# Other start addresses modulo 512 bytes for the weight buffers of a two-block transformer kernel

## The chip, the cores and the metric

The kernel runs on one core of a Trainium2 chip. The metric is the device time of one execution in microseconds (us). A partition of the on-chip memory (SBUF) is addressed in bytes; all addresses below are byte addresses within a partition, and "modulo 512" is the remainder that such an address leaves.

## The reference, cut to what matters

Two transformer blocks are computed for 256 tokens of width 1024, in float32, all of it in one launch. The first has a layer of gated spatial mixing beside latent attention, a layer of retention, and two SwiGLU networks of width 2816. The second has, twice, a SwiGLU of width 4096, a mixer of three branches (a gated delta rule, two banded attentions), and another SwiGLU of width 4096. By far the most work are matrix products of the 256 tokens with weights:

```python
def swiglu(h, w_gate, w_up, w_down):
    return (jax.nn.silu(h @ w_gate) * (h @ w_up)) @ w_down
```

## The kernel before, in words

**Weights.** All weights come as 772 chunks of at most 128 x 1024 float32 (512 KB), in the order in which TensorE uses them (the list `ORDER`). SyncE loads chunk c into slot c % 6 of `raw` (line 3269). ScalarE copies it, rounded to the short float32 format of TensorE (`float32r`), into slot c % 5 of `whi` (`upper`, line 1244). VectorE subtracts `whi` from `raw` and writes the rest, the lo part, into slot c % 5 of `wlo` (`lower`, line 2004). TensorE waits for `wlo` of the chunk, and ScalarE overwrites a slot only when TensorE has finished the chunk that stood there. A slot of `whi` or `wlo` has 4096 bytes, so all slots have the same start modulo 512; a block of 128 columns, which is what one weight load reads, has 512 bytes.

**Activations.** They are split in the same way. `xx` holds the normalised input of a product as 8 tiles k of 128 features, each with a hi part and a lo part of 256 tokens (1024 bytes each). `H` holds up to 32 such tiles of hidden values. `RX` is a third buffer of that kind, for the products that start before the layer norm's statistics are there; its hi and lo parts are 288 values apart and 258 columns of each are used. `Hs` is `H` shifted by 64 bytes, for the last down projection alone.

**Matmuls.** Every matmul goes through `mm`, and the profile gives all of them line 452. A matmul has a weight load of its own, of 128 columns of the stationary operand, and streams the other operand, the moving one. There are three forms:

- The pair (`mm2`): with the hi weights stationary, the hi and the lo part of a tile are streamed at once, 512 columns. Then, with the lo weights stationary, the hi part, 256 columns. It serves nearly all of the gate, up and down products of the SwiGLUs (`gemm_wide`, and the loop at line 679). The two halves of the result are added by VectorE.
- The triple (`mm3`): 256 columns three times, hi weights by hi part, lo weights by hi part, hi weights by lo part, all onto the same 256 columns of the result. It serves the projections of the mixers (`gemm_fm`, `gemm_acc`, `gemm_last`) and, with 258 columns from `RX`, the first products after a layer norm (`gemm_raw`).
- Token-major products (`gemm_tm`, `value`, `down_tokens`): the activations are stationary, and the weights are streamed, 512, 384 or 324 columns.

While a matmul streams its moving operand, the load of the next matmul's stationary operand runs beside it. So in a pair the lo weights are loaded while 512 columns from the start of an `xx` or `H` tile are streamed, and the next hi weights while 256 columns from the same start are streamed.

**Addresses.** `lay_memory` (line 242) places the buffers one behind the other. `line(p)` puts in a gap so that the next buffer starts at p modulo 512. All sizes of the buffers in question are multiples of 512 bytes. Before the change `raw` and `whi` start at 0 modulo 512, and `wlo`, `x`, `xx`, the scratch `t12` and `H` at 64. `Hs` starts 64 bytes behind `H`. `RX` starts 65664 bytes behind `H`, which is 128 modulo 512, its tiles k are 2304 bytes apart (256 modulo 512), and its lo part is 1152 bytes behind the hi part (128 modulo 512).

Of the kernel before, what the change touches and what calls it, by code (L numbers as in the profile page):

```python
# [7 lines left out]
F32R = mybir.dt.float32r  # L8
# [5 lines left out]
NRAW, NHL, CW = 6, 5, 1024  # L14
# [227 lines left out]
def lay_memory(nc, ctx, plan):  # L242
    m = Memory()

    def sb(name, shape, dt=F32):
        return ctx.enter_context(nc.sbuf_tensor(name, shape, dt))

    def line(past=0):

        gap = (past - nc.sbuf_base) % 512  # L250
        if gap:
            sb(f"gap{nc.sbuf_base}", [128, gap // 4])
        return nc.sbuf_base
# [13 lines left out]
    m.onc = nc.alloc_sbuf_tensor_at("onc", [128, 1], F32R, offset=on, align_bytes=64)[:, :]  # L267
    m.onr = m.onc.broadcast_to([128, 128])
    m.onm = m.onc.bitcast(F32).broadcast_to([128, 128])
    line(0)  # L270
    m.raw = sb("raw", [128, NRAW, CW])
    line(0)
    m.whi = sb("whi", [128, NHL, CW], F32R)
    line(64)
    m.wlo = sb("wlo", [128, NHL, CW], F32R)
    line(64)
    m.x = sb("x", [128, 8, 256])
    line(64)
    m.xx = sb("xx", [128, 8, 2, 256], F32R)
    m.xh, m.xl = m.xx[:, :, 0, :], m.xx[:, :, 1, :]  # L280
    at = line(64)
    t12 = sb("t12", [128, 2048 + 128])
    m.t1, m.t2 = (t12[:, 1024 * i:1024 * i + 1024].rearrange("p (a b) -> p a b", b=256) for i in range(2))
    blk = nc.alloc_sbuf_tensor_at("blk", [128, NBLK + 128], F32R, offset=at, align_bytes=64)
    m.pair = nc.alloc_sbuf_tensor_at("pair", [128, 256], F32R, offset=at + 6144, align_bytes=64)[:, :]
    m.E, m.eye16 = blk[:, 0:NBLK], blk[:, NBLK - 128:NBLK].bitcast(F32)
    m.Ph, m.Pl = blk[:, NBLK - 128:NBLK], blk[:, NBLK:NBLK + 128]
    at = line(64)
    left = nc.sbuf_bytes_remaining
    nar = min((left() if callable(left) else left) // 4 - 8 - 4096, 21696)  # L290
    region = sb("region", [128, 4096 + nar])
# [2985 lines left out]
def emit(nc, ins, out, plan):  # L3277

    with ExitStack() as ctx:
        m = lay_memory(nc, ctx, plan)  # L3280
        block = ctx.enter_context(nc.Block())

        @block.sync
        def _(e):
            sync_program(e, m, ins, out)

        @block.scalar
        def _(e):
            scalar_program(e, m, ins)

        @block.vector
        def _(e):
            vector_program(e, m)

        @block.gpsimd
        def _(e):
            gpsimd_program(e, m, ins)

        @block.tensor
        def _(e):  # L3300
            tensor_program(e, m)

        tables = {n: g.at for n, g in m.sig.items()}
        assert plan is None or plan == tables
        return tables
# [147 lines left out]
```

## Time and profile before

| | us |
|---|---|
| median of 3 runs | 2266.87 |
| lowest and highest | 2266.55, 2266.92 |
| the profiled execution's own time | 2266.66 |
| its span, first to last instruction | 2264.9 |
| TensorE busy in the span | 2251.1 |
| VectorE busy | 1781.2 |
| ScalarE busy | 1285.3 |

The profiled execution is a run of its own beside the three; 1.8 us of its time lie outside the span. "Busy" of TensorE is the union of all matmuls in flight, which overlap each other, so the mean duration of a matmul is not what it costs. What one costs is the distance from its start to the next one's start.

### The profile page before, as it was taken

To read this page: it belongs to the slowest core of one execution; us is meant where nothing else is said; L and a number is where in the kernel's file an instruction comes from. 1 tells how busy PE (TensorE), PEld (TensorE's weight loads), DVE (VectorE), ACT (ScalarE), POOL (GpSimd) and SP (SyncE) were. 2 spreads that over 40 slices of the span, in tenths; PEclk is the share of its full clock that TensorE was granted. 3 is DMA by queue.
4 is the path that set the end of the run, shared out by engine and by line. 5 is a ranking of instruction groups with operands and counts; after the bars stand their busy time and mean duration, and the time that the engine had idled before them with its cause. 6 is when DMAs were issued, how large, how long until landed. Compare 5 with 4: busy or idle time off the path is not lost.

```text
span 2264.9 us, 37643 instructions
## 1 busy us (share of the span) xinstructions
PE 2251.1 (99%) x15119; PEld 2047.7 (90%) x15119; DVE 1781.2 (79%) x2713; ACT 1285.3 (57%) x2016; POOL 79.4 (4%) x96
## 2 busy tenths in 40 slices
PE   9999999999999999999999999999999999999998
PEld 8988889998888888999999888998889999998887
DVE  7899658879858876897679886698768976798854
ACT  7855455655445555585666554466545856565542
POOL 0022000002100000020000000000000200000000
PEclk9999999999999999999999999999999999999999
DMA  7466565456556665654455555566665543556663
GB/s 244 132 199 196 193 211 176 150 159 215 184 186 214 195 192 191 204 178 129 133 172 193 197 194 190 168 203 206 195 194 197 180 133 122 182 182 221 190 185 100
DMA packets 115084, 412.45 MB, mean 182 GB/s; under 512 B 12896, under 2 KB 14304, under 8 KB 114656
## 3 DMA queue, kind: packets, MB, share of 16 engines
q1 hardware_dynamic: 114480, 407.77, 55.9%
q8 instruction: 120, 1.97, 0.4%
q0 software_dynamic: 288, 2.10, 0.3%
q14 instruction: 52, 0.43, 0.1%
q10 hardware_dynamic: 144, 0.18, 0.0%
HBM read 408.96 MB, written 1.05 MB: 181 GB/s over the span
## 4 chain that ended last, share of the span: by engine, by line
PE 88%; DVE 8%; ACT 2%; issue 1%; DMA 0%; SPq 0%; POOL 0%; DVEq 0%; ACTq 0%
PE ps L452 87%; DVE wlo L2004 3%; DVE region L2796 1%; ACT whi L1244 1%; ACT region L1466 1%; DMA raw<-in_ew_c 0%; PE ps L715 0%; DVE region L2323 0%; DVE RX L2193 0%; DVE x L2051 0%; DVE region L2326 0%; DVE x L2200 0%; DVE region L2439 0%; DVE region L2466 0%; DVE region L2965 0%
## 5 line engine op out<-in xcount | busy, mean ns | idle before, releaser
L452 PE MATMUL ps<-xx,whi 128*128 128x512 f32 (+1 forms) x4504 | 1286.2, 352 | 3.2 <-DVE wlo L2004 2.2
L2004 DVE TENSOR_TENSOR wlo<-raw,whi 128x1024 fp32r<-128x1024 f32 (+3 forms) x772 | 925.2, 1207 | 266.7 <-ACT whi L1244 265.7
L1244 ACT ACTIVATE whi<-raw 128x1024 fp32r<-128x1024 f32 (+3 forms) x772 | 801.1, 1043 | 491.3 <-PE ps L452 481.1
L452 PE MATMUL ps<-xx,wlo 128*128 128x256 f32 x3696 | 1025.0, 277 | 0.0
L452 PEld LDWEIGHTS ps<-xx,whi 128*128 128x128 f32 x4504 | 794.4, 188 | 120.2 <-issue 2.8
L452 PEld LDWEIGHTS ps<-xx,wlo 128*128 128x128 f32 x3696 | 693.8, 188 | 0.4
L452 PE MATMUL ps<-H,whi 128*128 128x512 f32 (+1 forms) x2144 | 571.6, 338 | 0.1
L452 PE MATMUL ps<-H,wlo 128*128 128x256 f32 x1632 | 453.7, 278 | 0.0
L452 PEld LDWEIGHTS ps<-H,whi 128*128 128x128 f32 x2144 | 370.7, 188 | 45.1 <-issue 0.6
L452 PEld LDWEIGHTS ps<-H,wlo 128*128 128x128 f32 x1632 | 306.7, 188 | 0.1
L1999 DVE TENSOR_REDUCE t<-ps 128x256 f32<-128x512 f32 x320 | 219.5, 688 | 31.6 <-PE ps L452 31.2
L1393 ACT ACTIVATE H<-t 128x256 fp32r<-128x256 f32 x140 | 58.6, 419 | 81.2 <-DVE t L2353 31.9
L1428 ACT ACTIVATE t<-t 128x256 f32<-128x256 f32 x160 | 65.5, 410 | 64.9 <-DVE t L2395 35.8
L452 PE MATMUL ps<-region 128*128 128x128 f32 (+9 forms) x944 | 89.4, 272 | 0.0
L452 PE MATMUL ps<-RX,whi 128*128 128x258 f32 x480 | 88.9, 284 | 0.0
L452 PEld LDWEIGHTS ps<-region 128*128 128x128 f32 (+5 forms) x944 | 75.8, 158 | 6.7
L452 PE MATMUL ps<-whi,Hs 128*128 128x512 f32 x256 | 79.8, 392 | 0.0
L452 PE MATMUL ps<-whi,xx 128*128 128x512 f32 (+1 forms) x288 | 79.3, 360 | 0.0
L452 PEld LDWEIGHTS ps<-RX,whi 128*128 128x128 f32 x480 | 75.3, 190 | 0.2
L3170 POOL TENSOR_TENSOR t<-t,R 128x256 f32<-128x256 f32 x44 | 53.3, 1211 | 549.1 <-ACT t L1428 549.1
L2022 DVE TENSOR_TENSOR H<-t,H 128x256 fp32r<-128x256 f32 x150 | 62.2, 419 | 9.0 <-ACT H L1393 5.8
L452 PE MATMUL ps<-RX,wlo 128*128 128x258 f32 x240 | 68.0, 283 | 0.0
(316 smaller groups left out, 1592.4 us busy)
## 6 DMA issues: line engine op xcount, KB each, us to landing
raw<-in_sg SPq DMA_DIRECT2D x128, 512.0 KB, 4.2
raw<-in_su SPq DMA_DIRECT2D x128, 512.0 KB, 4.2
raw<-in_sd SPq DMA_DIRECT2D x128, 512.0 KB, 4.4
raw<-in_mw_g SPq DMA_DIRECT2D x48, 512.0 KB, 3.7
raw<-in_fg SPq DMA_DIRECT2D x44, 512.0 KB, 4.1
raw<-in_fu SPq DMA_DIRECT2D x44, 512.0 KB, 4.2
raw<-in_fd SPq DMA_DIRECT2D x32, 512.0 KB, 3.6
raw<-in_mw_a SPq DMA_DIRECT2D x24, 512.0 KB, 4.2
```

What stands on the lines that cost most here:

```text
L452: return e.matmul(out, lhsT, rhs, start=start, stop=stop, skip_group_check=True)
L1244: e.activation(m.whi[:, c % NHL, 0:cw], m.raw[:, c % NRAW, 0:cw], ACT.Copy).then_inc(s["whi"].h, s["whi"].up(c))
L1393: e.activation(H[:, j, 0, :], m.t2[:, j % 4, :], ACT.Copy, scale=-0.5 if raw(j) else 1.0).then_inc(s["hhi"].h, s["hhi"].up(st, j))
L1428: e.activation(g, g, ACT.Silu).then_inc(s["silu"].h, s["silu"].up(st, j))
L1466: e.activation(S[:, i, sl], S[:, i, sl], ACT.Exp, bias=st[:, 1, c:c + 1], accum_out=st[:, 2, c:c + 1]).then_inc(s["aact"].h, s["aact"].up( ...
L1999: return e.tensor_reduce(dst, b[:, :].rearrange("p (a b) -> p b a", a=2), AX, ALU.add)
L2004: e.tensor_tensor(m.wlo[:, c % NHL, 0:cw], m.raw[:, c % NRAW, 0:cw], m.whi[:, c % NHL, 0:cw].bitcast(F32), ALU.subtract).then_inc(s["wlo"] ...
L2022: e.tensor_tensor(dst, src, hi.bitcast(F32), ALU.subtract).then_inc(s[sig[1]].h, s[sig[1]].up(*key))
L2796: e.scalar_tensor_tensor(y[:, d:256], pr[:, 0:256 - d], pk(f"cw{l}", 12 * (3 - d) + i), y[:, d:256], ALU.mult, ALU.add).then_inc(s["cdve"] ...
L3170: e.tensor_tensor(g, g, m.R[:, 0, :], ALU.mult).then_inc(s["fnrm"].h, s["fnrm"].up(st, j))
```

## The change

The order of the weight buffers becomes `raw`, `wlo`, `whi`. `raw` follows the constants with no gap, `wlo` starts at 128 modulo 512 and `whi` at 320. The `x`, `xx`, `t12` and `H` buffers start at 0. Relative to `xx` and `H`, `wlo` moves from 0 to +128 bytes, and `whi` from -64 to -192 bytes (320 - 512). No instruction, wait or transfer is added, removed or moved; only addresses differ.

```diff
--- before.py
+++ after.py
@@ -267,25 +267,24 @@
     m.onc = nc.alloc_sbuf_tensor_at("onc", [128, 1], F32R, offset=on, align_bytes=64)[:, :]
     m.onr = m.onc.broadcast_to([128, 128])
     m.onm = m.onc.bitcast(F32).broadcast_to([128, 128])
+    m.raw = sb("raw", [128, NRAW, CW])
+    line(128)
+    m.wlo = sb("wlo", [128, NHL, CW], F32R)
+    line(320)
+    m.whi = sb("whi", [128, NHL, CW], F32R)
     line(0)
-    m.raw = sb("raw", [128, NRAW, CW])
+    m.x = sb("x", [128, 8, 256])
     line(0)
-    m.whi = sb("whi", [128, NHL, CW], F32R)
-    line(64)
-    m.wlo = sb("wlo", [128, NHL, CW], F32R)
-    line(64)
-    m.x = sb("x", [128, 8, 256])
-    line(64)
     m.xx = sb("xx", [128, 8, 2, 256], F32R)
     m.xh, m.xl = m.xx[:, :, 0, :], m.xx[:, :, 1, :]
-    at = line(64)
+    at = line(0)
     t12 = sb("t12", [128, 2048 + 128])
     m.t1, m.t2 = (t12[:, 1024 * i:1024 * i + 1024].rearrange("p (a b) -> p a b", b=256) for i in range(2))
     blk = nc.alloc_sbuf_tensor_at("blk", [128, NBLK + 128], F32R, offset=at, align_bytes=64)
     m.pair = nc.alloc_sbuf_tensor_at("pair", [128, 256], F32R, offset=at + 6144, align_bytes=64)[:, :]
     m.E, m.eye16 = blk[:, 0:NBLK], blk[:, NBLK - 128:NBLK].bitcast(F32)
     m.Ph, m.Pl = blk[:, NBLK - 128:NBLK], blk[:, NBLK:NBLK + 128]
-    at = line(64)
+    at = line(0)
     left = nc.sbuf_bytes_remaining
     nar = min((left() if callable(left) else left) // 4 - 8 - 4096, 21696)
     region = sb("region", [128, 4096 + nar])
```

## Rows read from the trace of the kernel before

**Rows 1.** The page: span, TensorE busy time, TensorE clock in 40 slices.

```profile
span 2264.9 us, 37643 instructions
...
PE 2251.1 (99%) x15119; PEld 2047.7 (90%) x15119; DVE 1781.2 (79%) x2713; ACT 1285.3 (57%) x2016; POOL 79.4 (4%) x96
...
PEclk9999999999999999999999999999999999999999
```

**Rows 2.** Groups by line and shape, TensorE: busy us, mean ns, idle before.

```profile
L452 PE MATMUL ps<-xx,whi 128*128 128x512 f32 x2880 | 982.4, 390 | 0.0
...
L452 PE MATMUL ps<-H,whi 128*128 128x512 f32 x1120 | 381.2, 389 | 0.0
L452 PE MATMUL ps<-xx,whi 128*128 128x256 f32 x1616 | 301.7, 284 | 3.2 <-DVE wlo L2004 2.2 <-DVE xx L2059 1.1
L452 PE MATMUL ps<-H,whi 128*128 128x256 f32 x1024 | 190.4, 282 | 0.1
L452 PE MATMUL ps<-RX,whi 128*128 128x258 f32 x480 | 88.9, 284 | 0.0
L452 PE MATMUL ps<-whi,Hs 128*128 128x512 f32 x256 | 79.8, 392 | 0.0
...
L452 PE MATMUL ps<-whi,xx 128*128 128x512 f32 x160 | 50.4, 396 | 0.0
```

**Rows 3.** Waits of TensorE: us in total, times, longest.

```profile
PE ps L452 <- DVE wlo L2004: 2.2, 5, 1.0
```

**Rows 4.** Timeline of TensorE, a pair stretch: start us, us, instruction.

```profile
600.00 0.39 PE L452 MATMUL ps<-xx,whi 128*128 128x512 f32 x1
600.23 0.28 PE L452 MATMUL ps<-xx,wlo 128*128 128x256 f32 x1
600.34 0.39 PE L452 MATMUL ps<-xx,whi 128*128 128x512 f32 x1
...
610.43 0.28 PE L452 MATMUL ps<-H,wlo 128*128 128x256 f32 x1
```

**Rows 5.** Timeline of the weight loads in the same stretch.

```profile
600.00 0.19 PEld L452 LDWEIGHTS ps<-xx,wlo 128*128 128x128 f32 x1
```

**Rows 6.** Timeline of TensorE, a triple stretch on H.

```profile
1180.92 0.28 PE L452 MATMUL ps<-H,wlo 128*128 128x256 f32 x1
...
1191.17 0.28 PE L452 MATMUL ps<-H,wlo 128*128 128x256 f32 x1
```

**Rows 7.** Timeline of TensorE, a triple stretch on RX.

```profile
1460.77 0.28 PE L452 MATMUL ps<-RX,wlo 128*128 128x258 f32 x1
...
1461.13 0.28 PE L452 MATMUL ps<-RX,wlo 128*128 128x258 f32 x1
...
1461.48 0.28 PE L452 MATMUL ps<-RX,wlo 128*128 128x258 f32 x1
...
1461.85 0.28 PE L452 MATMUL ps<-RX,wlo 128*128 128x258 f32 x1
...
1471.93 0.28 PE L452 MATMUL ps<-RX,wlo 128*128 128x258 f32 x1
```

**Rows 8.** Timeline of TensorE, tokens against moving weights, xx stationary.

```profile
311.79 0.40 PE L452 MATMUL ps<-wlo,xx 128*128 128x512 f32 x1
...
326.55 0.40 PE L452 MATMUL ps<-wlo,xx 128*128 128x512 f32 x1
```

**Rows 9.** Timeline of TensorE, the same with Hs stationary.

```profile
2230.99 0.39 PE L452 MATMUL ps<-wlo,Hs 128*128 128x512 f32 x1
...
2248.33 0.39 PE L452 MATMUL ps<-wlo,Hs 128*128 128x512 f32 x1
```

**Rows 10.** Busy time by stretch: the pair stretch, then the triple stretch on H.

```profile
600.00:700.00 100.00, 100.00 (x591) 88.66 (x590) 66.74 (x91) 46.70 (x61) 1.29 (x1) 1.00 0.59 191
...
1180.50:1191.70 11.20, 11.20 (x97) 11.20 (x97) 11.20 (x26) 9.68 (x21) 0.00 (x0) 1.00 0.62 216
```

**Rows 11.** Groups of VectorE in the pair stretch, 600 to 700 us.

```profile
L2004 DVE TENSOR_TENSOR wlo<-raw,whi 128x1024 fp32r<-128x1024 f32 x31 | 37.9, 1222 | 27.0 <-ACT whi L1244 26.9
```

## The prediction

> **What bounds the kernel now.** I read the page first: TensorE is busy for 2251.1 of 2264.9 us, its clock is granted in full (2.4 GHz) in every slice [rows 1]. Then its waits: the longest in total, for lo weights, is 2.2 us [rows 3]. So nothing that feeds TensorE counts for much, and the time is the sum of the distances between matmul starts. The change touches no instruction. It can act only if the distance from one start to the next depends on where the operands lie.
>
> The groups by shape give the counts [rows 2]: 2880 + 1120 = 4000 pairs; (1616 + 1024)/2 = 1320 triples on xx and H, as each has two matmuls with hi weights; 480/2 = 240 triples on RX; token-major matmuls of 512 columns, three for every two with hi weights: 384 with Hs and 240 with xx stationary. The timelines give the distances, from the first to the last row and the number of repeats between (a row with x2 is two matmuls):
>
> - pair: 610.43 - 600.23 = 10.20 us for 30, **0.340 us** [rows 4]; 768 columns, so 0.443 ns per column.
> - triple on H: 10.25 us for 29, **0.3534 us** [rows 6]; also 768 columns.
> - triple on RX: 11.16 us for 31, **0.360 us** for 774 columns [rows 7].
> - token-major on xx: 14.76 us for 63 matmuls, **0.2343 us** for 512 columns [rows 8].
> - token-major on Hs: 17.34 us for 75, **0.2312 us** [rows 9].
>
> These sum to 1360 + 466 + 86 + 56 + 89 = 2057 us. The other 194 us of TensorE's busy time are matmuls on other tiles, other widths and the few waits; I cost the change on them at nothing, and leave them for the width of the range.
>
> **What can be gained.** The pair's rate is the fastest of the five. At 0.443 ns per column a triple would take 0.340, an RX triple 0.343 and a 512-column matmul 0.2267 us. The rest is excess: 1320 x 0.0134 = 17.7 us, 240 x 0.017 = 4.2 us, 240 x 0.0076 = 1.8 us, 384 x 0.0045 = 1.7 us, in all 25.4 us. In the pair the half of 512 columns is streamed beside a load at distance 0 (lo weights minus xx or H, modulo 512) and the half of 256 beside one at -64. The load of the lo weights starts together with the stream of the 512 [rows 4, 5]. The two halves take 0.23 and 0.11 us [rows 4], the same rate per column at two different distances. So I take the pair to be at its floor, and what can be gained is 25 us at most, 1.1%.
>
> **The change part by part.** Distances from the start of the moving operand to the start of what is loaded beside it, before and after, modulo 512:
>
> - Pair: lo load 0, becomes +128; hi load -64, becomes -192. Price unknown. From below: nothing, as it is at its floor. From above: the nearest rows in which 512 columns are streamed beside a load at +128 are those on Hs (Hs is 64 above H, hi weights 64 below it: +128 for two of three, +64 for the third), which cost 0.0045 us or 2.0% above the floor [rows 9]. On the pairs that would be 1360 x 0.020 = +27 us. With the 3.4% of xx [rows 8] it would be +46 us. I take nothing: the two halves of the pair show no difference between 0 and -64, and the token-major form on xx, where one load in three stands at the 0 that is free in the pair, has the larger excess of the two, so that the excess seems to belong to the form more than to the distance.
> - Triples on xx and H: the loads stand at 0, -64, -64 and become +128, -192, -192. These very distances are in the trace, in the RX triples: tile k of RX starts 128 + 256k above H, so the lo load there is at +128 for odd k and at -128 for even k, the first hi load at -192 for even k. What they show can be read in two ways. Per column, RX is slower (0.465 ns against 0.460). Per started 64 bytes (16 columns) it is faster: 258 columns touch 17, so 0.120 us is 7.06 ns each, as in the pair (0.340 over 48 is 7.08), while on H 0.3534 over 48 is 7.36. By the second reading a triple at the new distances loses its whole excess, -17.7 us; by the first it gains 0.005 ns x 768 x 1320, +5 us. The second gives one figure for two forms, and I lean to it, but its step at 258 columns rests on this one width. Between -17.7 and 0 I take half, -9 us.
> - RX: its distances become 0 or 256, 192 or -64, 64 or -192. The distances alternate with k by 256 already now, and the triples take 0.36, 0.35, 0.37 us in turn [rows 7] with no step of two, so I take nothing.
> - Token-major: the load of xx goes from +64, 0 to +192, -128, that of Hs from +128, +64 to +256, -64. Ends: -3.5 us (all of both excesses), and another 2% of 145 us, +3 us. I take 0.
> - Conversions: raw and whi both start at 0 now, and will not; the VectorE subtraction takes 1222 ns for a chunk [rows 11]. Cover: in the pair stretch VectorE is busy for 66.74 of 100 us [rows 10], so a subtraction could become half as long again before it bounds. In the triple stretch on H it is busy for all of 11.20 us [rows 10], but this work is run ahead by up to five slots. Without that cover each per cent on 772 subtractions of 1.2 us would be 9 us at the very most. I take 0.
> - The gaps and the order of the buffers by themselves: nothing, since no engine's work depends on them.
>
> Sum: -9 us. Against the profiled execution, 2266.66 (its span of 2264.9 and 1.8 us around it), that is 2257.7; the median of the runs is 0.2 us higher. I say 2258.
>
> The Trainium skill speaks against any effect: SBUF — State Buffer, "Who interferes with whom", states that only the port pair that VectorE and GpSimd share causes contention, and that TensorE has two independent read ports, for the moving operand and for the weight load. If that is all, start addresses move nothing and the sum is 0; it is weighed as the first rival.
>
> **The rivals.**
>
> 1. **No effect, 2266.9.** The triple could simply be bound by its loads. It has three loads in 0.3534 us, 0.118 each [rows 6], and the pair two in 0.340. If a load after a load costs 0.118 wherever it lies, the excess stays. For it: rows 6 and 7 are close (0.118 and 0.120), and rows 7 don't alternate with k. Against it: a bound by loads alone would give H and RX the same distance, and the same form (512 columns, ample time for the load) gives 0.2343 on xx and 0.2312 on Hs, whose distances differ by 64 bytes; something there depends on the address. The rule of the skill quoted above would give this case.
> 2. **Slower, 2294.** The pairs leave their floor. Stream and load would then collide at +128 and at -192 as they may do on Hs, and the stream is held up by 2.0%: +27 us. It decides as soon as a pair takes over 0.3422 us, since 4000 x 0.0022 is the 9 us of my gain; over 0.3411 the kernel is already slower if the triples gain nothing. For it: 0 and -64 are the two distances at which the pair is free, all others that the trace has come with an excess, and the pairs are 60% of the time. Against it: the larger excess of the two token-major forms is the one with a load at 0.
> 3. The conversions become the bound in the mixers: a part of the chance of slower, worth a few us.
>
> That the change does nothing because addresses end up elsewhere than it says is very unlikely: the line helper computes gaps from the actual base.
>
> **How the numbers follow.** Faster by the triples: 0.42, from 2241 (all 25.4 us) to 2262. No effect, which includes small gains and losses that cancel: 0.26. Slower: 0.32, of which most lies at +5 to +30 us. A difference of 0.2%, 4.5 us, is about what a measurement can tell from none. The range must take in both signs: 2243 leaves out the last 2 us of the full gain, 2296 holds the price of rows 9 on the pairs and leaves out that of rows 8. The faster case's own range is 2243 to 2262.
>
> **What the changed profile would show.** If right: a pair stretch still at 0.340 us per pair, triples on xx and H between 0.340 and 0.350, counts as before, no new waits of TensorE. If rival 1: all five distances as now. If rival 2: pairs at 0.343 to 0.350, which 30 pairs of a timeline tell at once. The conversions would show as longer rows of the subtraction and a wait of TensorE for lo weights far over 2.2 us. My forecast is wrong in its mechanism if the time falls while the triples stay at 0.353, or if the pair falls below 0.340.

## The result and the profile after

| | before | after |
|---|---|---|
| median, us | 2266.89 (6 runs) | 2309.45 (6 runs) |
| lowest and highest | 2266.55, 2272.03 | 2307.01, 2312.57 |
| profiled execution's own time | 2266.66 | 2312.57 |
| its span | 2264.9 | 2310.8 |
| TensorE busy | 2251.1 | 2296.7 |

The change makes the kernel slower: ratio 1.0186, 95% interval 1.0173 to 1.0199, 42.6 us on the medians. I had forecast 2258 us in a range of 2243 to 2296, with a chance of 0.32 for slower; 2309.45 lies outside the range. The profiled execution is at the upper end of the runs.

The page of the changed kernel, as in [rows 1]:

```profile
span 2310.8 us, 37643 instructions
...
PE 2296.7 (99%) x15119; PEld 2078.0 (90%) x15119; DVE 1786.1 (77%) x2713; ACT 1287.1 (56%) x2016; POOL 79.9 (3%) x96
...
PEclk9999999999999999999999999999999999999999
```

Instruction counts and clock are as before. The whole of the time is in TensorE's busy time, +45.6 of +45.9 us. The groups by line and shape, which answer to [rows 2] (the line numbers are one less after the change):

```profile
L451 PE MATMUL ps<-xx,whi 128*128 128x512 f32 x2880 | 1014.8, 394 | 0.0
...
L451 PE MATMUL ps<-H,whi 128*128 128x512 f32 x1120 | 393.6, 393 | 0.0
L451 PE MATMUL ps<-xx,whi 128*128 128x256 f32 x1616 | 302.7, 286 | 3.7 <-DVE wlo L2003 2.0 <-DVE xx L2058 1.5
L451 PE MATMUL ps<-H,whi 128*128 128x256 f32 x1024 | 191.0, 285 | 0.1
L451 PE MATMUL ps<-RX,whi 128*128 128x258 f32 x480 | 88.6, 284 | 0.0
```

Here is a way to read the cost of a pair from one row. The matmul of 512 columns is in flight for 394 ns (mean), longer than a whole pair takes, so the busy time of its group covers the pair stretches without a hole: busy time over count is the distance between pairs. On xx that is 982.4/2880 = 0.341 us before and 1014.8/2880 = 0.352 after, on H 381.2/1120 = 0.340 and 393.6/1120 = 0.351. Together +32.4 and +12.4, 44.8 us: the pairs are the whole loss. The triples' rows are up by 1.6 us together, RX is down by 0.3.

The waits of TensorE for lo weights, as in [rows 3], and VectorE's subtraction in the stretch of [rows 11]:

```profile
PE ps L451 <- DVE wlo L2003: 2.0, 4, 1.0
```

```profile
L2003 DVE TENSOR_TENSOR wlo<-raw,whi 128x1024 fp32r<-128x1024 f32 x28 | 34.3, 1225 | 28.4 <-ACT whi L1243 28.4
```

Neither moved. Then the timeline of the same pair stretch as [rows 4], the starts of five successive matmuls of 512 columns:

```profile
606.03 0.40 PE L451 MATMUL ps<-xx,whi 128*128 128x512 f32 x1
...
606.39 0.39 PE L451 MATMUL ps<-xx,whi 128*128 128x512 f32 x1
...
606.73 0.40 PE L451 MATMUL ps<-xx,whi 128*128 128x512 f32 x1
...
607.09 0.39 PE L451 MATMUL ps<-xx,whi 128*128 128x512 f32 x1
...
607.43 0.40 PE L451 MATMUL ps<-xx,whi 128*128 128x512 f32 x1
```

In the stretch of [rows 4] these starts were 0.34 us apart without exception. Now they are 0.36, 0.34, 0.36, 0.34: the pairs alternate. The section on patterns takes this up. In the tables that follow, a distance between starts is taken from all records of a form in the trace, each counted from its own start to the next matmul's start. They hold 4008 pairs: the 4000 of [rows 2], and eight more whose weights have 32 columns.

| form, sum of distances, us | before | after |
|---|---|---|
| pairs, 512-column half | 910.2 | 928.0 |
| pairs, 256-column half | 454.5 | 481.8 |
| triples on xx and H | 481.3 | 482.9 |
| triples on RX | 89.6 | 89.3 |
| token-major, 512 columns | 145.3 | 144.9 |

### The profile page after: what moved, and what is told of

Same layout as the page of the kernel before. It is cut to its first block, busy times and chain, and to the rows that moved or that the text cites. A ratio compares the mean times of both kernels' runs of the same rounds, so it can differ in the third digit from the quotient of the medians.

```text
span 2310.8 us, 37643 instructions
## 1 busy us (share of the span) xinstructions
PE 2296.7 (99%) x15119; PEld 2078.0 (90%) x15119; DVE 1786.1 (77%) x2713; ACT 1287.1 (56%) x2016; POOL 79.9 (3%) x96
## 4 chain that ended last, share of the span: by engine, by line
PE 88%; DVE 9%; ACT 2%; issue 1%; DMA 0%; SPq 0%; POOL 0%; DVEq 0%; ACTq 0%
PE ps L451 87%; DVE wlo L2003 3%; DVE region L2795 1%; ACT whi L1243 1%; DVE x L2199 0%; DMA raw<-in_ew_c 0%; PE ps L714 0%; ACT region L1465 0%; DVE region L2322 0%; DVE RX L2192 0%; DVE x L2050 0%; DVE region L2325 0%; DVE x L2221 0%; DVE region L2964 0%; DVE region L2431 0%
## 5 line engine op out<-in xcount | busy, mean ns | idle before, releaser
L451 PE MATMUL ps<-xx,whi 128*128 128x512 f32 (+1 forms) x4504 | 1319.6, 355 | 3.7 <-DVE wlo L2003 2.0
L451 PE MATMUL ps<-xx,wlo 128*128 128x256 f32 x3696 | 1039.3, 281 | 0.0
L451 PE MATMUL ps<-H,whi 128*128 128x512 f32 (+1 forms) x2144 | 584.6, 341 | 0.1
L451 PE MATMUL ps<-H,wlo 128*128 128x256 f32 x1632 | 458.5, 281 | 0.0
```

What stands on the lines that cost most here:

```text
L451: return e.matmul(out, lhsT, rhs, start=start, stop=stop, skip_group_check=True)
```

## The experiments

### One buffer at a time

Theory A: each half of a pair pays for the distance of the load beside it. Theory B: the two loads are coupled, and leaving either of the old distances costs the whole. Theory C: the distance of the hi weights does it all. Both kernels keep the changed order and gaps; all other buffers start at 0.

```diff
 (lo weights alone moved)
     line(128)
     m.wlo = sb("wlo", [128, NHL, CW], F32R)
-    line(320)
+    line(448)
     m.whi = sb("whi", [128, NHL, CW], F32R)
```

> The changed kernel with the hi weights put back to -64 from xx and H; only the lo weights stand at their new +128. In the changed kernel the pair takes 0.351 us against 0.340, and of these 11 ns about 4.5 lie in the half of 512 columns (beside which the lo weights are loaded) and about 7 in the half of 256 (beside which the hi weights are loaded). Theory A, each half pays for the distance of the load beside it: only the 512 half is longer, pair 0.345, time 2267 + 4000 x 0.0045 = 2285 us. Theory B, the two loads are coupled, and leaving either of the two old distances costs the whole: pair 0.351, 2309 us. Theory C, the lo distance is harmless and the hi distance does it all: 2267 us.

```diff
 (hi weights alone moved)
-    line(128)
-    m.wlo = sb("wlo", [128, NHL, CW], F32R)
     line(320)
     m.whi = sb("whi", [128, NHL, CW], F32R)
     line(0)
+    m.wlo = sb("wlo", [128, NHL, CW], F32R)
+    line(0)
```

> The changed kernel with the lo weights put back to 0 from xx and H (and behind the hi weights, as before the change); only the hi weights stand at their new -192. Theory A: only the half of 256 columns is longer, by 7 ns, pair 0.347, time 2267 + 28 = 2295 us. Theory B: pair 0.351, 2309 us. Theory C: 2309 us.

| | time, us | ratio to before | 512 half | 256 half |
|---|---|---|---|---|
| before | 2267.05 | | 0.2271 | 0.1134 |
| lo alone at +128 | 2288.96 | 1.0089 (1.0074 to 1.0104) | 0.2287 | 0.1184 |
| hi alone at -192 | 2303.99 | 1.0159 (1.0141 to 1.0176) | 0.2323 | 0.1175 |
| both (the change) | 2309.45 | 1.0186 (1.0173 to 1.0199) | 0.2315 | 0.1202 |

(The last two columns are mean distances between starts, in us, in the profiled execution.) Each move does harm by itself, +22 and +37 us, and the two together cost 43, not 59. All three theories fall. Against A: moving only the lo weights lengthens above all the 256-column half (by 5.0 ns), beside which the hi weights are loaded, at an unchanged distance. Against B: there are intermediate values. Against C: the lo weights alone cost 22 us.

### Order and absolute address

> The changed kernel's order of buffers (raw without a gap, lo weights ahead of hi weights) with the old distances: lo weights at 0 and hi weights at -64 from xx and H, everything 64 bytes further on modulo 512 than before. If only the distances between stationary and moving operands count (A, B and C alike): pair 0.340, 2267 us. If the order, the start of raw or absolute addresses have a part in the loss: above 2275 us.

```diff
     line(128)
     m.wlo = sb("wlo", [128, NHL, CW], F32R)
-    line(320)
+    line(64)
     m.whi = sb("whi", [128, NHL, CW], F32R)
-    line(0)
+    line(128)
     m.x = sb("x", [128, 8, 256])
 ...
```

The median is 2269.53 us, ratio 1.0003 (0.9991 to 1.0014), but no execution took that: five of the ten took 2266.9 to 2267.0 us and five 2272.1 to 2272.5. The kernel before has the same two levels, five of the thirteen executions beside it at the upper one; the section on the period of 256 comes back to them. The profile is one of the lower level and has the pairs at 0.340. The new order, `raw` without a gap and a shift of everything by 64 bytes cost nothing within that interval; the 43 us come from the distances.

### The grid of distances

```python
def pairs(lo, hi, reps=3, X=X):
    for _ in range(reps):
        b = bank()
        for k in range(8):
            c = k * 128
            mm(b[:, :], hi[:, c:c + 128], X[:, k].rearrange("p a b -> p (a b)"), k == 0, False)
            mm(b[:, 0:256], lo[:, c:c + 128], X[:, k, 0, :], False, True)
...
for i in range(8):
    for j in range(8):
        pairs(lo[i], hi[j])
```

> No part of the reference is computed: TensorE alone runs matmuls on prepared buffers while the other engines rest. For each of 8 x 8 combinations of start addresses modulo 512 in steps of 64 bytes (lo weights, hi weights; the moving operand at 0) it runs 24 pairs, then for each of 8 distances 24 matmuls of 512 and 24 of 256 columns with a load each, then 16 triples for each of the 64 combinations, and at last 48 pairs each at the old and the new distances with everything moved on by 64. Theory A: the time of a pair is a sum of one term for the lo distance and one for the hi distance; 0.340 at (0, -64), 0.351 at (+128, -192), 0.345 and 0.347 with one of the two moved; few other combinations are at 0.340. Theory B: 0.340 at a few combinations, 0.351 at all others, no intermediate values. If contention with VectorE and ScalarE was the cause, all combinations take 0.340 here, since those engines rest. If the absolute address counts, the last 48 + 48 pairs differ from the same distances in the grid.

First, matmuls of 512 columns alone, 24 in a row, each with a load of its own; the letters A to F behind `hi` are distances of 0, 64, 128, 192, 256 and 320 bytes. The timeline merges each run into one row: start, duration, count.

```profile
582.57 5.63 PE L179 MATMUL ps<-X,hiA 128*128 128x512 f32 x24
588.03 5.76 PE L179 MATMUL ps<-X,hiB 128*128 128x512 f32 x24
593.63 5.74 PE L179 MATMUL ps<-X,hiC 128*128 128x512 f32 x24
599.21 5.67 PE L179 MATMUL ps<-X,hiD 128*128 128x512 f32 x24
604.72 5.61 PE L179 MATMUL ps<-X,hiE 128*128 128x512 f32 x24
610.17 5.76 PE L179 MATMUL ps<-X,hiF 128*128 128x512 f32 x24
```

The starts of these runs are 5.46, 5.60, 5.58, 5.51 and again 5.45 us apart, over 24: 0.2275, 0.2333, 0.2325, 0.2296, 0.2271 us per matmul. Only TensorE is at work here, so no other engine's access can be the cause, and only the start of the weights differs from run to run: a stream is held up by the load beside it, by an amount that depends on their distance and repeats after 256 bytes. At distance 0 the 512 columns run at the rate of the pair, [rows 4], and 64 bytes further they take 2.5% more.

Matmuls of 256 columns with a load each behave otherwise:

```profile
626.85 3.02 PE L179 MATMUL ps<-X,hiA 128*128 128x256 f32 x24
629.70 2.99 PE L179 MATMUL ps<-X,hiB 128*128 128x256 f32 x24
632.53 3.01 PE L179 MATMUL ps<-X,hiC 128*128 128x256 f32 x24
```

These starts are 2.85 and 2.83 us apart, 0.1188 and 0.1179 us per matmul. At all eight distances it is 0.1175 to 0.1196; none reaches the 0.1134 of the pair's half of 256. So a 256-column matmul can be faster between other matmuls than among its like, and its time is not set by the distance of its own load alone.

Second, the pairs. The old distances (lo 0, hi 448 modulo 512) and the new ones (lo 128, hi 320), a lo matmul and the twentieth after it:

```profile
105.86 0.28 PE L179 MATMUL ps<-X,loA 128*128 128x256 f32 x1
...
112.66 0.28 PE L179 MATMUL ps<-X,loA 128*128 128x256 f32 x1
```

```profile
222.86 0.28 PE L179 MATMUL ps<-X,loC 128*128 128x256 f32 x1
...
229.86 0.28 PE L179 MATMUL ps<-X,loC 128*128 128x256 f32 x1
```

6.80 and 7.00 us, 0.340 and 0.350 a pair, with every other engine at rest. Moving everything by 64 bytes changed neither by more than 0.2 ns. The values are no sum of a term for each distance, as theory A has it: from lo 0 to lo 64 a pair goes from 340.0 to 346.6 ns at hi 192, and from 353.5 to 346.6 at hi 0. Over the 64 combinations the map repeats within 0.1 ns when the lo weights move by 256 bytes. When the hi weights do, it repeats within 0.2 ns for lo 0 and 64, but for lo 128 and 192 up to 3.6 ns lie between two such values (lo 128: hi 0 at 350.2, hi 256 at 346.6). The next section finds both values at one combination, after different starts. Third, the map of the triples modulo 256, in ns per triple (16 triples each, the first four left out):

```
triples         hi 0    hi 64   hi 128  hi 192
lo 0            360.0   353.3   355.0   353.3
lo 64           353.3   353.2   356.8   356.7
lo 128          357.1   354.8   356.2   346.7
lo 192          353.3   340.0   350.0   353.3
```

The old distances (lo 0, hi 192 modulo 256) give 353.3 and the new ones (lo 128, hi 64) 354.8, as in the whole kernel. And there is a combination at 340.0: the triple is not bound by its three loads.

One value of the grid did not fit. Lo 0, hi 320, the distances of the kernel with the hi weights alone moved, ran at 340.0 in the grid, while that kernel took 350 for most pairs. But that kernel's trace has the same loop over the same H in both ways. First the down projection at 1400 us, then the one at 1440; start of a lo matmul and of the thirtieth after it:

```profile
1399.74 0.28 PE L451 MATMUL ps<-H,wlo 128*128 128x256 f32 x1
...
1410.24 0.28 PE L451 MATMUL ps<-H,wlo 128*128 128x256 f32 x1
```

```profile
1439.80 0.28 PE L451 MATMUL ps<-H,wlo 128*128 128x256 f32 x1
...
1450.00 0.28 PE L451 MATMUL ps<-H,wlo 128*128 128x256 f32 x1
```

10.50 us against 10.20 for 30 pairs, 0.350 and 0.340, with the same buffers and the same code. Each value is kept up to an interruption: at 1428.9 us a single matmul on other tiles stands between the pairs, and those ahead of it take 0.350, those behind it 0.340, up to 1483.4 us, where matmuls on RX follow.

### Patterns and starts

Theory D: stream and loads lock into a repeating pattern; distances decide which patterns exist, the start of a stretch decides which of them is taken.

```python
def start(s):
    cols = (0, 128, 160, 258, 324, 384)[s]
    ...
    for k in range(2):
        mm(b[:, 0:cols], hi[0][:, k * 128:k * 128 + 128], ..., k == 0, k == 1)
...
for s in range(6):
    start(s)
    pairs(lo[i], hi[j], 2)
```

> No part of the reference is computed. Each of 4 x 4 combinations (lo, hi weights in steps of 64 bytes; the map of the grid repeats every 256 bytes) runs 16 pairs six times, each time after two matmuls of another width (none, 128, 160, 258, 324, 384 columns). Then triples for five combinations in the same way, and in a second part four combinations of pairs and two of triples while VectorE and ScalarE copy other buffers without a break. Theory D: matmuls and loads lock into a repeating pattern; the distances decide which patterns exist, the start of a stretch decides which of them is taken, and it is kept to the end of the stretch. Then lo 0, hi 192 (the old distances modulo 256) gives 0.340 after every start; lo 0, hi 64 (as in the run with the hi weights alone moved) gives 0.340 after some starts and 0.350 after others, and lo 128, hi 64 (the new distances) gives values between 0.344 and 0.356. The second part gives the same values as the first. Theory E: the other engines' reads and writes push the pair off its floor, and the real kernel's 0.350 where the grid has 0.340 comes from them. Then all starts give 0.340 for lo 0, hi 64 in the first part, and 0.350 in the second.

Lowest and highest mean of a pair over the six starts, in ns, the first four pairs of each stretch left out:

```
pairs    hi 0            hi 64           hi 128          hi 192
lo 0     346.6 to 353.6  340.0 to 353.0  351.5 to 352.5  340.0 to 350.0
lo 64    346.5 to 346.7  353.3 to 353.4  346.6 to 346.7  346.6 to 353.4
lo 128   346.6 to 350.2  349.5 to 353.3  350.4 to 351.5  346.6 to 353.3
lo 192   346.6 to 350.7  352.6 to 353.4  346.5 to 353.4  348.7 to 353.2
```

Theory E falls. Of theory D, that the distances decide which patterns exist and the start decides among them holds; that the old distances give 340.0 after every start does not. Lo 0, hi 64 took 340.0 twice in six and 349.9 to 353.0 else. The new distances took 349.5 to 353.3: 340 was not among the patterns after any start, and one of them alternates 344 and 356, the 0.34 and 0.36 of the timeline above. The old distances took 340.0 after five starts, and 350.0 after one, which I had not expected. Lo 128, hi 0 took 350.2 after two starts and 346.6 after four, the two values of the grid. With VectorE and ScalarE copying other buffers meanwhile, the values are the same ones (old distances 340.0 five times and 350.0 once; lo 128, hi 192 at 346.6 to 346.7, without the one 353.3); only which start leads to which changes here and there. The triple at lo 192, hi 64 took 340.0 after all six starts, with the other engines at rest and again with ScalarE copying (VectorE's last copy ended at 949.8 us, when this stretch had just begun). At the new distances the triple took 354.5 to 354.8.

### A period of 256

> The changed kernel with lo weights at +256 and hi weights at +192 from xx and H (raw still without a gap): other than the old distances (0 and -64) modulo 512, equal to them modulo 256. The grid shows a period of 256 bytes, by which the pair takes 0.340 us and the kernel 2267 us. If only distances modulo 512 count, as the change's own description has it, these are distances like any other, and the pair is at 0.345 to 0.355, 2285 to 2310 us.

```diff
     line(128)
-    m.wlo = sb("wlo", [128, NHL, CW], F32R)
-    line(320)
     m.whi = sb("whi", [128, NHL, CW], F32R)
-    line(0)
+    line(192)
+    m.wlo = sb("wlo", [128, NHL, CW], F32R)
+    line(448)
     m.x = sb("x", [128, 8, 256])
 ...
```

Two of its ten executions took 2266.9 us and eight 2272.0 to 2272.5; ratio 1.0015 (1.0005 to 1.0024). The executions of the kernel before have the same two levels: eleven of the thirteen beside it at 2266.7 to 2267.1, two at 2271.9. The profile is one of the upper level (2272.23). Its long pair stretches are at 0.340, but for one of 503 pairs from 114 to 290 us and 15 pairs just ahead of it; thirty of the 503:

```profile
119.98 0.28 PE L451 MATMUL ps<-xx,wlo 128*128 128x256 f32 x1
...
130.48 0.28 PE L451 MATMUL ps<-xx,wlo 128*128 128x256 f32 x1
```

10.50 us, 0.350 a pair; 503 pairs x 10 ns are the 5 us between the levels. In the profile of the kernel before and in that of the section on order, both of the lower level, the same stretch is at 0.340. So the period of 256 holds, and the change's "modulo 512" is twice the true period. The second pattern of the old distances, seen after one start in six above, makes the upper level here. That it does so in the kernel before too is likely from the equal times, but no profile of its upper level exists. Whether eight of ten at the upper level against two of thirteen is an effect of the layout stays open as well; the ratio of 1.0015 comes from these shares, as the lower level is the same.

### Finer steps, and token-major

```python
for j in range(16):
    pairs(lo[0], hi[j])      # hi in steps of 16 bytes
```

> No part of the reference is computed. Pairs with lo weights at 0 and hi weights in 16 steps of 16 bytes, then hi at 192 and lo in 16 steps, then triples with both moved together (hi 128 above lo), then token-major matmuls of 512 columns for 4 x 4 starts of the moving weights, with the stationary activations at 0 and at 64. If conflicts are counted in units of 64 bytes, the values change in steps of four starts; if in finer units, the floor of 0.340 is narrower or wider than 64 bytes. Token-major: the excess over 0.2267 us changes with the start of the weights, and the set with the activations at 64 is the set at 0 moved by one step.

With lo at 0, hi at 0, 16, ... 240 bytes, a pair takes, in ns, the first eight of each combination left out: 353.3, 351.4, 351.5, 353.1, 353.1, 350.1, 350.1, 352.0, 352.0, 349.3, 349.3, 340.0, 340.0, 344.5, 344.5, 353.3. Values come in twos, so the unit is 32 bytes and not the 64 that I had named, and 340.0 holds at 176 and 192 only. The same twos appear with lo moved at hi 192, with one exception: lo 0 took 340.0 and lo 240 took 350.0, the two values that the old distances have after different starts. Of the triples with hi 128 above lo, only lo 176 and 192 took 340.0; the others took 353.4 to 363.4. Token-major matmuls run at 226.7 ns when hi and lo weights start where the stationary activations do, modulo 256, and at 228.9 to 234.5 at the other fifteen combinations; with the activations at 64 the floor moves with them, to hi 64, lo 64. The combinations of [rows 8] and [rows 9] stand at 234.5 and 231.1 in this map. Those of the changed kernel (hi 64, lo 128 and hi 0, lo 64) stand at 232.2 and 232.1, so the map also accounts for the token-major row of the table in the first section, which hardly moved.

### A version that places each chunk by its form

Pairs, triples and token-major products want three different distances. A slot that is 256 bytes longer than its chunk can give each chunk its own start. That costs 2560 bytes, which are taken from `raw` (five buffers for six). The control has the longer slots and five raw buffers, with all chunks at the old distances (and `raw` without a gap).

```diff
-NRAW, NHL, CW = 6, 5, 1024
+NRAW, NHL, CW = 5, 5, 1024
+SLOT = CW + 64
...
+SHIFT = {"pair": (192, 0), "triple": (64, 192), "token": (0, 0), "token Hs": (64, 64), "RX": (192, 0)}
+
+def slot(buffer, which, c):
+    at = c % NHL * SLOT + SHIFT[form(*ORDER[c])][which] // 4
+    return buffer[:, at:at + CW]
...
-        return m.whi[:, c % NHL, :], m.wlo[:, c % NHL, :]
+        return slot(m.whi, 0, c), slot(m.wlo, 1, c)
```

(The shifts are hi, lo; `form` tells from a chunk's name which form uses it; the copies of ScalarE and VectorE use `slot` too. The control has (192, 0) for all.)

> The kernel before with five raw buffers for six, and with slots of whi and wlo that are 4096 + 256 bytes apart; all chunks at the old distances modulo 256. Distances are as before, so pairs 0.340, triples 0.3535. One raw buffer less may delay some transfers: 2267 to 2275 us. If slot spacing modulo 512 counts (it is 256 now, so every second slot stands 256 bytes off), the pairs leave 0.340 and the time goes above 2275.

> The control, but each chunk is placed within its slot by the form that uses it: pairs lo 0, hi 192 (as before), triples lo 192, hi 64, token-major chunks with hi and lo at the start of the stationary activations, all modulo 256. Theory D (distances decide the pattern; the grid's values hold in the whole kernel): triples 0.340 instead of 0.3535 (1320 x 0.0135 = -17.8 us), token-major 0.2267 instead of 0.2343 and 0.2312 (-3.5 us), pairs unchanged: 21 us below the control, about 2246 us. If the other engines' work or the starts of short stretches break the patterns in the real kernel, triples stay between 0.345 and 0.354 and less than half of it comes.

> The same, and the chunks used with RX have lo at +64 from xx, which is +192 from RX's hi part, with hi at +64 from it: the triple's best combination as far as RX's hi part goes; its lo part stands 128 bytes off. If the first two matmuls of the triple decide, RX goes from 0.360 towards 0.343, up to 4 us less than the run before; if the third counts as much, it may as well get slower, by up to 2 us.

| | time, us | ratio to before |
|---|---|---|
| control | 2272.26 (2267.03 to 2272.47) | 1.0005 (0.9994 to 1.0016) |
| by form | 2255.92 (2255.83 to 2255.99) | 0.9944 (0.9927 to 0.996) |
| by form, RX too | 2256.15 (2256.00 to 2256.28) | 0.9945 (0.993 to 0.996) |

The control shows the two levels again and nothing else: six of its ten executions are at the upper one, its profile too (2272.24), and there the same stretch from 114 us on is at 0.350. By form, the kernel is 11 us faster than before, 2255.92 where about 2246 was expected: about half of the expected 21 us. Its groups, and 34 triples on H:

```profile
L478 PE MATMUL ps<-xx,whi 128*128 128x512 f32 x2880 | 982.6, 390 | 0.2 <-DVE wlo L2030 0.2
...
L478 PE MATMUL ps<-H,whi 128*128 128x512 f32 x1120 | 381.2, 389 | 0.0
L478 PE MATMUL ps<-xx,whi 128*128 128x256 f32 x1616 | 294.2, 281 | 4.3 <-DVE wlo L2030 2.6 <-ACT region L1726 0.5 <-DVE xx L2085 0.5
L478 PE MATMUL ps<-H,whi 128*128 128x256 f32 x1024 | 184.6, 279 | 0.8 <-DVE H L2048 0.4 <-DVE region L2800 0.2
L478 PE MATMUL ps<-RX,whi 128*128 128x258 f32 x480 | 89.4, 285 | 0.4 <-DVE RX L2219 0.4
```

```profile
1162.02 0.28 PE L478 MATMUL ps<-H,wlo 128*128 128x256 f32 x1
...
1173.58 0.28 PE L478 MATMUL ps<-H,wlo 128*128 128x256 f32 x1
```

Pairs are at 0.341 and 0.340, and these triples at 11.56/34 = 0.340. Summed over the trace, the triples on xx and H went from 481.3 to 470.3 us (-11.0; expected -17.8), the token-major ones of 512 columns from 145.3 to 141.9 (-3.4, as expected). More than a fifth of the triples did not reach 340: of the 1320, 1033 took 339 to 341 ns, and the rest took other patterns in short stretches, changed over to another form, or waited. In the kernel before, none took under 348. RX lost 1.1 us and the small matmuls 1.3, probably because the faster triples come to their inputs earlier. TensorE's waits show part of that:

```profile
PE ps L478 <- DVE wlo L2030: 2.8, 8, 0.8
PE ps L741 <- ACT region L1498: 1.5, 3, 0.6
...
PE ps L478 <- ACT region L1726: 0.5, 2, 0.2
```

In the kernel before, the wait for lo weights was 2.2 us [rows 3] and the other two are 1.1 and below what is listed. The shift for RX changed nothing for the better: 120.9 ns per matmul against 120.0, waits left out, and 91.2 us in all against 90.7. That its first two matmuls decide is not borne out.

## Why the prediction was wrong

- **What bounds the kernel: right.** TensorE's start distances are the time, and nothing else moved.
- **The step that failed: "I take the pair to be at its floor" and then "I take nothing".** The floor was right: no combination went below 340.0 ns. What failed is the price of leaving it. I argued that 0 and -64 are equally free, so the pair does not care; the grid shows that the combination (0, -64) is one of the few that are free (of the 16 combinations modulo 256, only lo 0 with hi 64 or hi 192 reach 340.0, the first after some starts, the second after most), and that every other costs 6.5 to 13.6 ns. Two points at the floor were no sample: they were one combination.
- **The bound from above was right and I did not use it.** Rows 8 and 9 priced the excess at 3.4% and 2.0% of the pairs, +46 and +27 us; measured, 44.8 us in the trace and 42.6 on the medians. The 512-column half alone went from 0.2271 to 0.2315 us, which is the 2.0% of [rows 9]; the 256-column half, which I had no row to price by, lost 6.0%, 27.3 of the 45 us. So the +46 of xx comes so near by luck: neither half lost 3.4%. The price of the nearest row would have given 2294 as the forecast, still 15 us short. My range ended at 2296 because I left the xx rows out.
- **The objection that carried the decision was false.** I said that the larger token-major excess comes with a load at distance 0, so the excess belongs to the form. The map of token-major shows it belongs to the combination: with both weights at the activations' start it is gone (226.7), and one of the two at distance 0 is not enough.
- **Triples: -9 us forecast, +1.6 measured.** Of the two readings of RX, the one per column, +5 us, had the sign right. The one per started 64 bytes, to which I leaned, gives 340 at the new distances, where the grid has 354.8; its one figure for two forms was a coincidence at 258 columns. That a triple can lose its excess was right (340.0 at lo 192, hi 64), but not at the new distances. The bound by loads of rival 1 falls with it, though 256-column matmuls with a load each do take its 0.118 when they stand alone.
- **RX with no step of two in k, so no effect: right outcome, wrong reason.** Its tiles alternate by 256 bytes, which is exactly the period. I read it as insensitivity, where it was the period showing.
- **No effect (rival 1, 0.26) fell.** The rule that I quoted from the Trainium skill, SBUF — State Buffer, "Who interferes with whom", does not hold in this case: with all other engines at rest, the load beside a stream changes the stream's time by up to 2.7% with its address. The measurement decides.
- **Rival 2 is what happened**, at 0.32: the pairs left their floor, and its threshold (a pair over 0.3411 us) was passed by ten times the margin. Its size was too small: it had 0.343 to 0.350 us a pair and 2294, where 0.351 to 0.352 and 2309.45 were measured.
- **Conversions, gaps, order: nothing, right.** The subtraction takes 1225 ns after and 1222 before.

## What to carry to other kernels

When TensorE is busy without a hole, measure start distances by form and compare them per column: a form above the rate of the best one may be held up by the weight load beside it. Choose the start addresses of stationary and moving buffers together, by combinations that were measured, not one buffer at a time, and check several starts of a stretch. A flat part of one combination in a trace says nothing about its neighbours; a row with an excess at another distance is the better price.

## What was not expected

- A float32r stream of 512 columns takes 0.2267 us at best (0.443 ns a column at a granted clock of 2.4 GHz) and 0.2333 beside a load 64 bytes off. The period is 256 bytes, the unit 32 bytes. A matmul of 256 columns took 0.1134 us in the pair and in the best triple, and 0.1175 to 0.1196 among its like.
- Stream and loads fall into patterns that last until the stretch is interrupted, 503 pairs in one case. The same code on the same buffers ran at 0.340 and at 0.350 us a pair in one execution, and two levels of a kernel's time, 5 us apart, come from one such stretch, as the profiles of the run with the period of 256 and of the control show.
- What exactly collides (a bank, a shared path, a buffer before the array) stays open; the runs show only that it happens with TensorE alone at work, that it depends on where the load stands against the stream, and how.
